# Norms by halves in a two-block transformer kernel: roots, weight splits and a fourth result moved among the chunks

## What is computed

```python
def rms_norm(x, g):
    xf = x.astype(jnp.float32)
    y = xf * lax.rsqrt(jnp.mean(xf * xf, axis=-1, keepdims=True) + RMS_EPS)
    return (y * g.astype(jnp.float32)).astype(x.dtype)
...
    for layer in range(DEPTH_2):
        ...
        h = h + rms_norm(m, g[1])
        f = sq_relu_mlp(rms_norm(h, g[2]), w_up[layer], w_down[layer])
        h = h + rms_norm(f, g[3])
```

## Time and profile before

| | us |
|---|---|
| median of 3 runs (lowest, highest) | 2759.64 (2756.28, 2759.88) |
| the profiled execution | 2760.13 |
| its span, first to last instruction | 2758.4 |
| TensorE matmuls busy | 2635.8 (96%) |
| VectorE busy | 1824.0 (66%) |
| ScalarE busy | 1044.2 (38%) |
| POOL busy | 946.5 (34%) |

### The profile page before, as it was taken

The page is one execution under the profiler, slowest core; times in us unless marked ns, Lnnn a source line. Parts: engine busy times, 40 slices in busy tenths (PEclk is TensorE's granted clock), DMA queues, the critical chain, the costliest instruction groups (busy, mean ns, idle before and its releaser), DMA issues.

```text
span 2758.4 us, 37590 instructions
## 1 busy us (share of the span) xinstructions
PE 2635.8 (96%) x14417; PEld 2371.7 (86%) x14417; DVE 1824.0 (66%) x3139; ACT 1044.2 (38%) x1695; POOL 946.5 (34%) x532
## 2 busy tenths in 40 slices
PE   8799999899999999999999899999999989999998
PEld 6668899899999999999999877888889756888887
DVE  5644799988888878888888645670735055590542
ACT  5333334345555543333333343422223254522221
POOL 2323410014444442333333135344442422344442
PEclk9899999999999999999999899999999999999999
DMA  3222236569999988999999422233331321233331
GB/s 132 92 84 71 91 107 190 158 194 309 347 346 351 329 309 299 350 348 337 344 350 346 137 91 84 77 98 94 97 95 62 107 84 54 70 109 97 95 97 54
DMA packets 235473, 488.47 MB, mean 177 GB/s; under 512 B 85128, under 2 KB 135192, under 8 KB 235040
## 3 DMA queue, kind: packets, MB, share of 16 engines
q1 hardware_dynamic: 198432, 351.83, 39.8%
q0 software_dynamic: 36864, 134.23, 13.4%
HBM read 442.98 MB, written 42.88 MB: 176 GB/s over the span
## 4 chain that ended last, share of the span: by engine, by line
PE 81%; DVE 14%; ACT 2%; issue 1%; DMA 1%; POOL 0%; SPq 0%; DVEq 0%; ACTq 0%
PE ps L293 25%; PE ps L294 24%; PE ps L295 24%; PE ps L1644 3%; DVE wl L282 2%; PE ps L462 1%; DVE ti L1504 1%; DVE ti L1499 1%; DVE hT L2167 1%; PE ps L2410 1%; DVE tv L1502 1%; PE ps L2495 1%; DVE oh L1590 1%; DVE slot L1602 1%; DVE sR L1500 1%
## 5 line engine op out<-in xcount | busy, mean ns | idle before, releaser
L274 ACT ACTIVATE wh<-wraw 128x1024 fp32r<-128x1024 f32 x487 | 513.1, 1058 | 1291.5 <-PE ps L295 1287.3
L293 PE MATMUL ps<-Xh,wh 128*128 128x512 f32 (+2 forms) x2312 | 864.9, 374 | 40.3 <-DVE wl L282 12.8
L282 POOL TENSOR_TENSOR wl<-wraw,wh 128x1024 fp32r<-128x1024 f32 x231 | 562.1, 2438 | 946.5 <-ACT wh L274 946.5
L294 PE MATMUL ps<-Xl,wh 128*128 128x512 f32 (+2 forms) x2312 | 822.5, 356 | 0.0
L295 PE MATMUL ps<-Xh,wl 128*128 128x512 f32 (+2 forms) x2312 | 820.9, 355 | 0.0
L293 PEld LDWEIGHTS ps<-Xh,wh 128*128 128x128 f32 x2312 | 442.9, 192 | 87.9 <-issue 19.5
L294 PEld LDWEIGHTS ps<-Xl,wh 128*128 128x128 f32 x2312 | 443.5, 192 | 38.0
L295 PEld LDWEIGHTS ps<-Xh,wl 128*128 128x128 f32 x2312 | 441.2, 191 | 40.6
L282 DVE TENSOR_TENSOR wl<-wraw,wh 128x1024 fp32r<-128x1024 f32 x256 | 312.3, 1221 | 141.7 <-ACT wh L274 141.6
L293 PE MATMUL ps<-Hh,wh 128*128 128x384 f32 x1024 | 346.6, 338 | 8.0 <-DVE Hl L1854 8.0
L294 PE MATMUL ps<-Hl,wh 128*128 128x384 f32 x1024 | 345.6, 337 | 0.0
(11 more groups left out here) (307 smaller groups left out, 3353.9 us busy)
## 6 DMA issues: line engine op xcount, KB each, us to landing
wraw<-in_uT SPq DMA_DIRECT2D x128, 512.0 KB, 5.1
wraw<-in_v SPq DMA_DIRECT2D x128, 512.0 KB, 5.5
wraw<-in_up SPq DMA_DIRECT2D x128, 512.0 KB, 3.6
gA_scratch<-gl SPq DMA_DIRECT2D x122, 192.0 KB, 5.6
gl<-gA_scratch SPq DMA_DIRECT2D x122, 192.0 KB, 5.4
gG_scratch<-gbuf SPq DMA_DIRECT2D x64, 256.0 KB, 7.8
lg<-gG_scratch SPq DMA_DIRECT2D x128, 128.0 KB, 5.4
wraw<-in_w_q SPq DMA_DIRECT2D x24, 512.0 KB, 3.6
```

The source lines that it names most:

```text
L274: act.activation(wh[:, n % 4, :], wraw[:, n % 4, :], ACT.Copy).then_inc(s_wh, 1)
L282: pool.tensor_tensor(wl[:, n % 4, :], wraw[:, n % 4, :], wh[:, n % 4, :].bitcast(F32), ALU.subtract).then_inc(s_wl, 1)
L293: pe.matmul(o, ah, bh, start=start, stop=False)
L294: pe.matmul(o, ah, bl, start=False, stop=False)
```

## The change

In `last_halves` the root's sums stand after chunk per + 1 (2, or 3 where a result has 16 chunks) and the spreading after chunk per + 5 of m 6 (6, or 7). In `second_root` the spreading stands after chunk 5. `first_halves` takes a fourth result, `late`: its first half is made beside the second half of the first three, its second half after them. VectorE makes the low parts of four tiles of `W_K` and of the third and fourth tiles of `F0` and `F1` between its chunks; POOL's ranges end earlier. On ScalarE the high part of the fifth tile stands ahead of the squares, that of the sixth and seventh after square 3 and square 7. Root and spreading of the new norm stand one result later, after results 4 and 5, and results 5 and 6 use banks 6 and 5.

```diff
     def split_lo(pool, n):
...
-        if n in (4, W_U + 4, A_V):
+        if n in (4, W_U + 4, A_V, F0 + 2, F0 + 4, W_K, W_K + 4, F1 + 2, F1 + 4):
             pool.wait_ge(s_wl, n)
...
+    B_FU = {0: lin_banks(5) + [6, 5] + lin_banks(25), 1: None}
+    B_K = lin_banks(5) + [6, 5] + lin_banks(1)
-    B_O2 = [7, 2, 3, 0, 1, 4, 2, 3, 0, 1]
+    B_O2 = [7, 2, 3, 0, 1, 4, 3, 0, 1, 2]
...
+        def chunk(g, hf, kc):
+            ts, w, cs = HALF[hf], (tile0 + g) % 4, slice(kc * 128, kc * 128 + 128)
+            if hf == 0 and kc == 0:
+                pe.wait_ge(s_wl, tile0 + g + 1)
+            mm = three(pe, ps[banks[g]][:, ts], wh[:, w, cs], wl[:, w, cs], Xh[:, kc, ts], Xl[:, kc, ts], kc == 0, kc == 7)
+            if hf and kc == 7:
+                mm.then_inc(s_wuse, 1)
         for hf in range(2):
             for kc in range(8):
                 pe.wait_ge(*x[8 * hf + kc])
                 for g in group:
+                    chunk(g, hf, kc)
                 if hf == 0 and beside and kc in beside:
                     beside[kc](pe)
+                if hf and late is not None:
+                    if kc == 0:
+                        bank_free(pe, banks[late])
+                    chunk(late, 0, kc)
+        if late is not None:
+            for kc in range(8):
+                chunk(late, 1, kc)
...
-                    if hf and m == 6 and kc == 3:
+                    if hf and m == 6 and kc == per + 1:
                         root_pe(pe, name, root, 0)
-                    if hf and (m, kc) == ((7, 1) if per == 1 else (6, 11)):
+                    if hf and m == 6 and kc == per + 5:
                         spread_pe(pe, name, spread[0], read(0), 0)
...
-    def second_root(name, read, root=1, spread=4):
+    def second_root(name, read, root=1, spread=5):
...
-                      {0: lambda: last(1, 7), 3: lambda: root_act(act, "mo", 5, 1.0 / 1024, 1),
-                       5: lambda: split_hi(act, F0 + 3)})
+                      {0: lambda: last(1, 7), 1: lambda: split_hi(act, F0 + 3),
+                       4: lambda: root_act(act, "mo", 5, 1.0 / 1024, 1)}, F0)
...
+    def norm_beside(dve, name, tile0):
+        return {0: lambda: split_lo(dve, tile0 + 2), 4: lambda: split_lo(dve, tile0 + 3),
+                5: lambda: root_dve(dve, name, 1)}
...
+        split_hi(act, tile0 + 4)
         for c in range(8):
             sum_square(act, name, c, hT[:, c, :])
+            if c in (3, 7):
+                split_hi(act, tile0 + 5 + c // 4)
...
-                pe_linear(pe, t0, [3], bu, None, done)
+                pe_linear(pe, t0, [4], bu, None, done)
                 root_pe(pe, up, 5)
-                pe_linear(pe, t0, [4], bu, None, done)
+                pe_linear(pe, t0, [5], bu, None, done)
                 spread_pe(pe, up, 7, (s_kept, N[up].kept + 1))
...
-            fold_norm_act(act, "k", "kv", 0, t0 + 16,
-                          {0: lambda: square(1, 6), 2: lambda: split_hi(act, W_K + 2), 4: second_7, 7: lambda: root(1)})
+            fold_norm_act(act, "k", "kv", 0, t0 + 16, {0: lambda: split_hi(act, W_K + 1), 2: second_6, 5: second_7,
+                                                       7: lambda: root(1)}, W_K)
...
             add_norm_dve(dve, sq_, fo, 24, "k", "kv", 0,
-                         {0: lambda: last(1, 6), 4: lambda: last(1, 7), 7: lambda: root_dve(dve, sq_, 1)})
+                         {0: lambda: split_lo(dve, W_K), 2: second_6, 3: lambda: split_lo(dve, W_K + 2),
+                          5: lambda: last(1, 7), 7: second_root_k})
```

More of the change, by code:

```diff
@@ L332, in pe_linear @@
             if halves:
-                first_halves(pe, tile0, group, banks, x, beside)
+                first_halves(pe, tile0, group, banks, x, beside, late)
             for q in range(0 if halves else per):
@@ L349, in pe_linear @@
                         each(group[-1], kc)
+            if halves and late is not None:
+                group.append(late)
             for g in group:
@@ L352, in pe_linear, with first_halves @@
             i += len(group)
-    def first_halves(pe, tile0, group, banks, x, beside):
+    def first_halves(pe, tile0, group, banks, x, beside, late):
+        def chunk(g, hf, kc):
[5 more added lines that the diff above has]
+                mm.then_inc(s_wuse, 1)
         for hf in range(2):
-            ts = HALF[hf]
             for kc in range(8):
@@ L361, in first_halves @@
                 for g in group:
-                    if hf == 0 and kc == 0:
-                        pe.wait_ge(s_wl, tile0 + g + 1)
-                    w, cs = (tile0 + g) % 4, slice(kc * 128, kc * 128 + 128)
-                    mm = three(pe, ps[banks[g]][:, ts], wh[:, w, cs], wl[:, w, cs], Xh[:, kc, ts], Xl[:, kc, ts], kc == 0,
-                               kc == 7)
-                    if hf and kc == 7:
-                        mm.then_inc(s_wuse, 1)
+                    chunk(g, hf, kc)
                 if hf == 0 and beside and kc in beside:
                     beside[kc](pe)
+                if hf and late is not None:
[5 more added lines that the diff above has]
+                chunk(late, 1, kc)
     def last_halves(pe, name, tile0, banks, done, read, root=5, spread=(6, 7), xh=None, xl=None, kcs=8):
@@ L2012, in gmlp_pool @@
             x_lo(pool, "ao", c, mo[:, c, :])
-        for n in range(A_O + 4, A_O + 12):
+        for n in range(A_O + 4, A_O + 10):
             split_lo(pool, n)
@@ L2132, in gmlp_dve @@
         root_dve(dve, "mo", 0)
-        add_norm_dve(dve, "mo", uT, 8, "up0", "g2", 16, {4: lambda: root_dve(dve, "mo", 1)}, s_mo)
+        add_norm_dve(dve, "mo", uT, 8, "up0", "g2", 16, norm_beside(dve, "mo", F0), s_mo)
         for c in range(1, 7):
@@ L2207, in ffn_pool @@
         t0 = (F0, F1)[layer]
-        for n in range(t0 + 4, t0 + 68):
+        for n in range(t0 + 4, t0 + 64):
             split_lo(pool, n)
@@ L2218, in ffn_pe @@
             if half == 0:
-                pe_linear(pe, t0, [0, 1, 2], bu, XL[up], done, first=(0, 1, 2),
-                          beside=second_root(*(("mo", hg_read("mo")) if layer == 0 else ("o2", hg_read("o2")))))
-                pe_linear(pe, t0, [3], bu, None, done)
+                pe_linear(pe, t0, [0, 1, 2, 3], bu, XL[up], done, first=(0, 1, 2),
+                          beside=second_root(*(("mo", hg_read("mo")) if layer == 0 else ("o2", hg_read("o2")))), late=3)
+                pe_linear(pe, t0, [4], bu, None, done)
                 root_pe(pe, up, 5)
-                pe_linear(pe, t0, [4], bu, None, done)
+                pe_linear(pe, t0, [5], bu, None, done)
                 spread_pe(pe, up, 7, (s_kept, N[up].kept + 1))
-                pe_linear(pe, t0, list(range(5, 16)), bu, None, done)
+                pe_linear(pe, t0, list(range(6, 16)), bu, None, done)
             else:
@@ L2242, in ffn_act @@
             if half == 0:
-                for m in range(4):
-                    split_hi(act, t0 + m + 4)
+                split_hi(act, t0 + 7)
                 root_act(act, up, 5, 1.0 / 1024)
@@ L2274, in ffn_act, with second_6 @@
             split_hi(act, W_K)
-            split_hi(act, W_K + 1)
+            def second_6():
+                square(1, 6)
+                split_hi(act, W_K + 2)
             def second_7():
@@ L2327, in ffn_dve, with second_6, second_root_k @@
         if layer == 0:
+            def second_6():
+                last(1, 6)
+                split_lo(dve, W_K + 1)
+            def second_root_k():
+                split_lo(dve, W_K + 3)
+                root_dve(dve, sq_, 1)
             add_norm_dve(dve, sq_, fo, 24, "k", "kv", 0,
-                         {0: lambda: last(1, 6), 4: lambda: last(1, 7), 7: lambda: root_dve(dve, sq_, 1)})
+                         {0: lambda: split_lo(dve, W_K), 2: second_6, 3: lambda: split_lo(dve, W_K + 2),
+                          5: lambda: last(1, 7), 7: second_root_k})
             for c in range(1, 7):
@@ L2393, in att_pool @@
             x_lo(pool, "o2", c, qTs[:, c, :])
-        for n in range(W_O2 + 4, W_O2 + 12):
+        for n in range(W_O2 + 4, W_O2 + 10):
             split_lo(pool, n)
@@ L2522, in att_pe @@
     def att_pe(pe):
-        pe_linear(pe, W_K, [0, 1, 2], B_K, XL["k"], lambda g: (s_ke, g + 1), first=(0, 1, 2),
-                  beside=second_root("f0", hg_read("f0")))
-        pe_linear(pe, W_K, [3], B_K, None, lambda g: (s_ke, g + 1))
+        pe_linear(pe, W_K, [0, 1, 2, 3], B_K, XL["k"], lambda g: (s_ke, g + 1), first=(0, 1, 2),
+                  beside=second_root("f0", hg_read("f0")), late=3)
+        pe_linear(pe, W_K, [4], B_K, None, lambda g: (s_ke, g + 1))
         root_pe(pe, "k", 5)
-        pe_linear(pe, W_K, [4], B_K, None, lambda g: (s_ke, g + 1))
-        spread_pe(pe, "k", 6, (s_kept, N["k"].kept + 1))
-        pe_linear(pe, W_K, [5, 6, 7], B_K, None, lambda g: (s_ke, g + 1))
+        pe_linear(pe, W_K, [5], B_K, None, lambda g: (s_ke, g + 1))
+        spread_pe(pe, "k", 7, (s_kept, N["k"].kept + 1))
```

(6 more changed lines are left out.)

14 lines of the change are left out of this document (6 added, 8 removed).

## The result

The changed kernel takes **2764.72 us** (median of 9 runs, 2762.10 to 2770.26) beside 2756.12 of the kernel before (9 runs, 2750.96 to 2759.88): 1.0033 of its time, 95% interval 1.0024 to 1.0041. It is slower by 8.6 us, where 2755.5 was forecast.

What follows compares the result with a forecast made beforehand. TensorE was taken as the bound (81% of the chain). Seam gains 2.3 + 0.8 + 2.5 - 0.4 = 5.2 us, less 1.1 for the clock, net 4.1: from 2760.13 to 2756.0, less 0.5: 2755.5 us; range 2751 to 2760.5.

Steps and rivals of the forecast that it cites:

- (a) to (c): First half of seam mo: earlier root and spreading, VectorE's splits; first wait 1.5 instead of 2.0 us, gain 2.6 us.
- mo: Seam where one layer's normed result feeds the next layer's matmuls, ahead of an up projection; claimed gain 2.3 us.
- (d): Second half of seam mo with the late result: no TensorE waits, 14.5 us until result 3 is whole, gain 0.7 us.
- (e): Behind mo's second half: a new wait of 1.0 us for the summed squares before the root, bounds 0 and 2.5.
- o2: Another such seam, by the same steps as mo but without its low clock; claimed gain 0.8 us.
- f0: Another such seam: waits for `wl` and `kTs` go, 1.5 us before the second root comes; claimed gain 2.5 us.
- clock allowance: One of three new 1.5 us waits followed by 3.3 us at 1.2 GHz: 1.1 us lost, bounds 0 and 4.8.
- Seam q: Seam with only root and spreadings moved: POOL's piece of `Xl` stands behind a later split, cost 0.4 us.
- The end: End of the kernel (f1): spreading 1.44 us earlier, but VectorE still waits for m 6, so gain 0.
- The anchor: Time of the kernel before from which the forecast was counted: median of its runs, 2759.64 us.
- Rival 3: Slower: long stretches at 1.2 GHz after the root's wait in three seams, 10 us lost, 2769 us; chance 0.06.
- signs of being wrong: Root waits over 2.5 us, fifth tile's `wl` late, or clock 0.50 for over 4 us in a seam other than q.

Runs made afterwards that it cites:

- e7: The change, but with seam q's root and spreadings back where they stood: 1.0024 of the time of the kernel before.
- e8: The change, but VectorE's squaring of the relu in the up projections covers 8 columns instead of 512: 1.0024 of the kernel before.
- e3: The change, but in the up projections the new norm's sums and spreading one result later still, after results 5 and 6: 1.0062 of the kernel before.
- e1: The change without its late fourth result, ScalarE's squares ahead of the fifth tile and the new norm's root and spreading placed as before: 0.9999 of the kernel before.
- e2: The change, but the new norm's sums and spreading inside result 5, after its chunks 2 and 4: 1.0017 of the kernel before.
- e4: The kernel before with the change's banks and, in the up projections alone, sums and spreading after results 4 and 5: 1.0042 of the kernel before.
- b0_before_again: A second profile of the unchanged kernel before: 2755.17 us.
- a1: The changed kernel measured once more, nothing altered: median 2764.99 us, 1.0033 of the kernel before.
- e5: The change, but sums after chunk 3 of result 4, spreading after result 4, and ScalarE's fifth tile after square 3: 0.9985 of the kernel before.

## Why the prediction was wrong, point by point

- **(a) to (c), first halves: right in size.** Waits of 1.60, 1.60 and 1.52 us for 1.5; the second half of mo starts 13.2 us after the old layer's last product where before it was 16.2, a gain of 3.0 for 2.6. VectorE's two held additions are back at 0.43. And as written, "most of the earlier start is given back to the wait for `wh`": VectorE's first operation is early, then idle for 1.12 us.
- **(d), the late result: right.** No waits in the second half, and 14.6 us to a whole result 3 for 14.5.
- **(e), the root wait: right in size (1.04 for 1.0), wrong in what it costs.** The step "I take 1.0" counted the wait alone. Behind it the clock fell in mo and o2 in all four profiles that hold the change's seams (the change twice, e7, e8), and result 5 then took 6.8 to 8.5 us instead of 5.5. In f0 the same wait stands in five profiles (e3 too), and the clock fell behind it in one, the change's first. The prediction had put low clock only behind the waits of 1.5. In mo and o2 it never came there (full clock in all nine profiles that have the 1.60), in f0 behind the 1.52 in two of nine, e1 and e2. Its "clock allowance" was of about the right size for one seam and stood at the wrong wait. Seam f0 from 2143 to 2149 us in the change's first profile; from 2146 to 2152 in its second, and e1 from 2111 to 2114, behind the 1.52:

```profile
2143.00:2149.00 6.00, 6.00 (x19) 5.03 (x20) 0.18 (x1) 1.84 (x3) 6.00 (x3) 0.50 0.39 101
```
```profile
2146.00:2152.00 6.00, 6.00 (x33) 5.17 (x34) 0.18 (x1) 2.30 (x4) 5.79 (x3) 1.00 0.33 96
```
```profile
2111.00:2114.00 3.00, 3.00 (x16) 3.00 (x16) 0.89 (x2) 0.00 (x0) 0.00 (x0) 0.50 0.28 79
```

- **The step that was missing: the later spreading was given no price.** Moving root and spreading one result on delays all of VectorE's work for the up projection. The parts (a) to (e) price the root's wait ("Queued behind it are result 5 and all that follows. I take 1.0"), and then treat the rest as before. The trace of before had what was needed: VectorE back to back from the spreading to the last `Fl`, 3.8 us to spare there, and a move that takes a result's 5.5 us from them. That leaves 1.7 us of wait in each layer, 1.79 measured, and low clock behind it in one. Measured 3.6 and 2.1 us. This is the largest part of the loss, and e4 shows it alone.
- **Seam q: "Cost 0.4 us", measured about 4** (against `b0_before_again`; 3.7 to 5.1 timed). The wait grew by 0.65. Against TensorE's last old product VectorE's addition of the second half's m 6, ScalarE's copy and POOL's split all shift by 0.44, as worked out; the rest is the piece of `Xl` that POOL makes, which takes 0.95 us where it took 0.73. The clock took the other 3.3. The prediction knew that this seam fell to 1.2 GHz behind 1.95 us, took that for its normal state, and so saw no more to lose. It was the state of two executions in five.
- **f0: gain as worked out** (no wait for `wl`, 1.52 for 1.5 ahead of the second root, none for `kTs` at result 5), before the clock behind its root wait. With o2 it makes 2.0 to 2.2 us where f0's clock stayed full (a1, e7), for 2.5 + 0.8.
- **The end: 0, right.** It waits 1.67 us there as it did before with 1.66.
- **The anchor** was 2759.64, where later medians are near 2756. Measured from there the forecast would have been 2752, so it hides 3.6 us of the miss: a gain of 4.1 us stood against a loss of 8.6.
- **Rivals.** Rival 3, slower through low clock behind the root's wait, had the sign and half of the mechanism, at 0.06. It priced ten microseconds at 1.2 GHz after every root wait, 5.1 us lost; result 5 lost 1.3 to 3.0. No rival had VectorE's backlog in the up projection. Of the signs of being wrong, "0.50 stands for more than 4 us in a seam other than q" did occur, in f0 in the change's first profile, and not in its second, so it doesn't mark the cause. The signs for the single steps nearly all came true: each was about a seam, and over half the loss lies outside them.

The Trainium skill, page TensorE: Matmul & The Clock Gate, section Why this matters for your kernels, warns, of idle gaps, only of longer ones than these. The traces don't agree for the waits of 2.60, 2.0, 1.79 and 1.04 us here: behind each of them the rows show a clock below full in at least one seam.

## To carry to other kernels

When an operation that releases a backlog (here a normalising factor) is moved later, take the consumer with the tightest slack behind it and follow it to its last use: pace of the catching-up engine with its held operations, pace of the consumer, and slack at the last item. Where sums would have to wait for their data, put them between chunks of a result whose data are long there: in e2 and e5 the wait and the low clock behind it were gone, and with the spreading back at its old place too, e5 was 13 us faster than the change (1.0033 to 0.9985). Before building on a low-clock stretch in one profile, look at a second one: it may be the exception, and the usual case may have more to lose.
